# Two halves of the tokens in turns: another column order for TensorE's products, undone by VectorE

## The reference

```python
def first_block(x, mem, ...):
    # layer a: differential attention (6 heads of 2 x 64) + attention to 256 memory rows
    h = _rmsnorm(x, a_norm_attn)
    z = h @ a_w_in                                   # q, k, v, memory q
    x = x + concat([o_self, o_mem]) @ a_w_out
    x = x + relu(_rmsnorm(x, a_norm_mlp) @ a_w_up) ** 2 @ a_w_down      # 1024 -> 4096 -> 1024
    # layer b: the same with 12 causal heads; k and v from w_kv, q from b_w_in
    return _rmsnorm(x, final_norm)

def second_block(x, ...):
    # layer sb: stick-breaking attention, 16 heads of 64; layer fox: forgetting attention
    q, k, v = split(a @ w_qkv); h = h + rmsnorm(merge(o) @ w_o, post_g)
    # after each: a gated MLP with a causal convolution of 3 taps over the tokens
    f = conv_ffn(rmsnorm(h, ffn_pre_g), w_up, conv_w, conv_b, w_down)   # 1024 -> 2 x 2816 -> 1024
    h = h + rmsnorm(f, ffn_post_g)
```

## Time and profile before

| | us |
|---|---|
| median of three runs | 1201.98 |
| lowest and highest | 1201.56, 1206.76 |
| the profiled execution | 1206.9 |
| its span in the trace | 1205.1 |
| TensorE busy | 1188.5 |
| VectorE busy | 892.2 |
| ScalarE busy | 759.7 |
| GpSimd busy | 326.8 |

### The profile page before, as it was taken

How to read it: one execution, slowest core, us unless ns; L and a number is a source line. 1 busy time by engine, 2 the same in 40 slices (tenths; PEclk the granted TensorE clock), 3 DMA queues, 4 the chain that set the end, 5 groups by cost and what they waited for, 6 DMA issues and landing times.

```text
span 1205.1 us, 26850 instructions
## 1 busy us (share of the span) xinstructions
PE 1188.5 (99%) x9150; PEld 1105.7 (92%) x9150; DVE 892.2 (74%) x1491; ACT 759.7 (63%) x1373; POOL 326.8 (27%) x303
## 2 busy tenths in 40 slices
PE   9999999999999999999999999999999999999998
PEld 8888999999988999999998789999878988999986
DVE  7788877655578877666569979987456776999953
ACT  7666655444555655455557788887456665988842
POOL 3320355300012255432202105433000210455500
PEclk9999999999999999999999999999999999999999
DMA  8554465566545465655643345555645743566662
GB/s 319 176 155 145 162 206 192 177 206 202 198 144 156 151 196 194 217 185 190 209 157 118 136 152 192 191 186 192 198 139 170 241 134 125 189 195 204 194 209 89
DMA packets 64055, 216.64 MB, mean 180 GB/s; under 512 B 7776, under 2 KB 10992, under 8 KB 63984
## 3 DMA queue, kind: packets, MB, share of 16 engines
q1 hardware_dynamic: 63808, 215.17, 54.6%
q10 hardware_dynamic: 176, 0.54, 0.2%
HBM read 211.47 MB, written 1.06 MB: 176 GB/s over the span
## 4 chain that ended last, share of the span: by engine, by line
PE 87%; DVE 9%; ACT 2%; issue 1%; DMA 1%; POOL 0%; SPq 0%; DVEq 0%; ACTq 0%; POOLq 0%
PE bank L773 16%; PE bank L775 16%; PE bank L774 16%; PE bank L700 4%; PE bank L701 4%; PE bank L702 4%; PE bank L649 4%; PE bank L650 3%; PE bank L651 3%; DVE w_lo L1589 3%; PE bank L578 2%; PE bank L579 2%; PE bank L584 2%; PE bank L920 1%; PE bank L903 1%
## 5 line engine op out<-in xcount | busy, mean ns | idle before, releaser
L1127 ACT CAST w_hi<-raw 128x1024 fp32r<-128x1024 f32 x386 | 403.1, 1048 | 282.8 <-PE bank L775 129.5
L1589 DVE TENSOR_TENSOR w_lo<-raw,w_hi 128x1024 fp32r<-128x1024 f32 x386 | 504.4, 1316 | 88.6 <-ACT w_hi L1127 88.3
L773 PE MATMUL bank<-h_hi,w_hi 128*128 128x256 f32 x1184 | 329.7, 278 | 0.2
L775 PE MATMUL bank<-h_hi,w_lo 128*128 128x256 f32 x1184 | 328.5, 277 | 0.0
L774 PE MATMUL bank<-h_lo,w_hi 128*128 128x256 f32 x1184 | 328.5, 277 | 0.0
L773 PEld LDWEIGHTS bank<-h_hi,w_hi 128*128 128x128 f32 x1184 | 223.7, 189 | 1.1 <-DVE h_lo L1662 1.0
L774 PEld LDWEIGHTS bank<-h_lo,w_hi 128*128 128x128 f32 x1184 | 222.3, 188 | 0.1
L775 PEld LDWEIGHTS bank<-h_hi,w_lo 128*128 128x128 f32 x1184 | 222.3, 188 | 0.0
L773 PE MATMUL bank<-a_hi,w_hi 128*128 128x256 f32 x544 | 150.6, 277 | 1.1 <-DVE a_lo L1662 1.0
L775 PE MATMUL bank<-a_hi,w_lo 128*128 128x256 f32 x544 | 150.2, 276 | 0.0
L774 PE MATMUL bank<-a_lo,w_hi 128*128 128x256 f32 x544 | 150.2, 276 | 0.0
(11 more groups left out here) (222 smaller groups left out, 2108.5 us busy)
## 6 DMA issues: line engine op xcount, KB each, us to landing
raw<-in_w_up_sb SPq DMA_DIRECT2D x44, 512.0 KB, 3.5
raw<-in_w_up_fox SPq DMA_DIRECT2D x44, 512.0 KB, 4.2
raw<-in_w_up_a SPq DMA_DIRECT2D x32, 512.0 KB, 3.5
raw<-in_w_down_a SPq DMA_DIRECT2D x32, 512.0 KB, 4.6
raw<-in_w_up_b SPq DMA_DIRECT2D x32, 512.0 KB, 4.1
raw<-in_w_down_b SPq DMA_DIRECT2D x32, 512.0 KB, 4.6
raw<-in_w_in_sb SPq DMA_DIRECT2D x24, 512.0 KB, 3.7
raw<-in_w_in_fox SPq DMA_DIRECT2D x24, 512.0 KB, 3.6
```

Of the source, the lines that this page charges most:

```text
L773: nc.tensor.matmul(dst, w_hi[:, slot, w], src_hi[:, at + k, :], start=begin, stop=False)
L775: last = nc.tensor.matmul(dst, w_lo[:, slot, w], src_hi[:, at + k, :], start=False, stop=end)
L1127: nc.scalar.copy(w_hi[:, slot, 0:k * P], raw[:, slot, 0:k * P]).then_inc(hi_ready, 1)
L1589: nc.vector.tensor_tensor(w_lo[:, slot, 0:k * P], raw[:, slot, 0:k * P], w_hi[:, slot, 0:k * P].bitcast(f32), ALU.subtract).then_inc(lo_re ...
```

## The change

The moving operand of every feature-major product gets another order of columns. `in_turns` turns a tile's 256 tokens into the order 0, 128, 1, 129, ... 127, 255: the two halves of 128 tokens in turns. The matmul still writes its columns to PSUM one after the other, so a bank now holds the tokens in that order. Each eviction puts them back: it reads PSUM in two runs of 128 columns with a step of two (`product`), beside the two contiguous halves of its other operand and of its destination (`halves_of`). All buffers in SBUF keep their layout. Token-major products, attention, norms and transposes are not changed. No instruction is added, removed or put elsewhere.

```diff
+        def in_turns(x):
+            return x.rearrange("p (h a) -> p a h", h=2)
+        def halves_of(x):
+            return x.rearrange("p (h a) -> p h a", h=2)
+        def product(b):
+            return bank[b][:, 0:TOK].rearrange("p (a h) -> p h a", h=2)
...
-                            nc.tensor.matmul(dst, w_hi[:, slot, w], src_hi[:, at + k, :], start=begin, stop=False)
-                            nc.tensor.matmul(dst, w_hi[:, slot, w], src_lo[:, at + k, :], start=False, stop=False)
-                            last = nc.tensor.matmul(dst, w_lo[:, slot, w], src_hi[:, at + k, :], start=False,
+                            nc.tensor.matmul(dst, w_hi[:, slot, w], in_turns(src_hi[:, at + k, :]), start=begin, stop=False)
+                            nc.tensor.matmul(dst, w_hi[:, slot, w], in_turns(src_lo[:, at + k, :]), start=False, stop=False)
+                            last = nc.tensor.matmul(dst, w_lo[:, slot, w], in_turns(src_hi[:, at + k, :]), start=False,
                                                     stop=end)
...
-                nc.vector.tensor_tensor(dst, bank[s % 2][:, 0:TOK], scale[:], ALU.mult).then_inc(tile_out, 1)
+                nc.vector.tensor_tensor(halves_of(dst), product(s % 2), halves_of(scale[:]),
+                                        ALU.mult).then_inc(tile_out, 1)
...
-                    x = X[:, i * per + b, :]
-                    src = bank[OUT_BANK[b]] if name.startswith("out") else bank[b]
-                    nc.vector.tensor_tensor(x, src[:, 0:TOK], x, ALU.add).then_inc(tile_out, 1)
+                    x = halves_of(X[:, i * per + b, :])
+                    nc.vector.tensor_tensor(x, product(b), x, ALU.add).then_inc(tile_out, 1)
...
-                    nc.vector.scalar_tensor_tensor(u_buf[:, b, :], bank[b][:, 0:TOK], 0.0, rstd[:], ALU.max,
-                                                   ALU.mult).then_inc(tile_out, 1)
+                    nc.vector.scalar_tensor_tensor(halves_of(u_buf[:, b, :]), product(b), 0.0, halves_of(rstd[:]),
+                                                   ALU.max, ALU.mult).then_inc(tile_out, 1)
```

More of the change, by code:

```diff
@@ L648, in query_key_tile @@
                     dst, slot = bank[s % 2][:, 0:TOK], unit % RING
-                    nc.tensor.matmul(dst, w_hi[:, slot, w], src_hi[:, k, :], start=k == 0, stop=False)
-                    nc.tensor.matmul(dst, w_hi[:, slot, w], src_lo[:, k, :], start=False, stop=False)
-                    last = nc.tensor.matmul(dst, w_lo[:, slot, w], src_hi[:, k, :], start=False, stop=k == KT - 1)
+                    nc.tensor.matmul(dst, w_hi[:, slot, w], in_turns(src_hi[:, k, :]), start=k == 0, stop=False)
+                    nc.tensor.matmul(dst, w_hi[:, slot, w], in_turns(src_lo[:, k, :]), start=False, stop=False)
+                    last = nc.tensor.matmul(dst, w_lo[:, slot, w], in_turns(src_hi[:, k, :]), start=False, stop=k == KT - 1)
                 last.then_inc(units_done, 1)
@@ L720, in out_part @@
                     w = slice(k * P, (k + 1) * P)
-                    nc.tensor.matmul(dst, w_hi[:, slot, w], o_hi[:, k, :], start=k == MEMORY_K[0], stop=False)
-                    nc.tensor.matmul(dst, w_hi[:, slot, w], o_lo[:, k, :], start=False, stop=False)
-                    last = nc.tensor.matmul(dst, w_lo[:, slot, w], o_hi[:, k, :], start=False, stop=k == LAST_K)
+                    nc.tensor.matmul(dst, w_hi[:, slot, w], in_turns(o_hi[:, k, :]), start=k == MEMORY_K[0], stop=False)
+                    nc.tensor.matmul(dst, w_hi[:, slot, w], in_turns(o_lo[:, k, :]), start=False, stop=False)
+                    last = nc.tensor.matmul(dst, w_lo[:, slot, w], in_turns(o_hi[:, k, :]), start=False, stop=k == LAST_K)
                     if k == LAST_K:
@@ L737, in out_tiles @@
                         w = slice(k * P, (k + 1) * P)
-                        nc.tensor.matmul(dst, w_hi[:, slot, w], o_hi[:, k, :], start=k == 0, stop=False)
-                        nc.tensor.matmul(dst, w_hi[:, slot, w], o_lo[:, k, :], start=False, stop=False)
-                        last = nc.tensor.matmul(dst, w_lo[:, slot, w], o_hi[:, k, :], start=False, stop=k == KT - 1)
+                        nc.tensor.matmul(dst, w_hi[:, slot, w], in_turns(o_hi[:, k, :]), start=k == 0, stop=False)
+                        nc.tensor.matmul(dst, w_hi[:, slot, w], in_turns(o_lo[:, k, :]), start=False, stop=False)
+                        last = nc.tensor.matmul(dst, w_lo[:, slot, w], in_turns(o_hi[:, k, :]), start=False, stop=k == KT - 1)
                     last.then_inc(units_done, 1)
@@ L793, in together @@
                             dst, slot = bank[s][:, 0:TOK], (g["unit"] + s) % RING
-                            nc.tensor.matmul(dst, w_hi[:, slot, w], src_hi[:, k, :], start=k == 0, stop=False)
-                            nc.tensor.matmul(dst, w_lo[:, slot, w], src_hi[:, k, :], start=False, stop=False)
+                            nc.tensor.matmul(dst, w_hi[:, slot, w], in_turns(src_hi[:, k, :]), start=k == 0, stop=False)
+                            nc.tensor.matmul(dst, w_lo[:, slot, w], in_turns(src_hi[:, k, :]), start=False, stop=False)
                         pe.wait_ge(h_lo, operand_count(name, 0, 0, k))
@@ L798, in together @@
                             dst, slot = bank[s][:, 0:TOK], (g["unit"] + s) % RING
-                            last = nc.tensor.matmul(dst, w_hi[:, slot, w], src_lo[:, k, :], start=False,
+                            last = nc.tensor.matmul(dst, w_hi[:, slot, w], in_turns(src_lo[:, k, :]), start=False,
                                                     stop=k == KT - 1)
@@ L1035, in _ @@
                 dst = bank[6][:, 0:TOK]
-                nc.tensor.matmul(dst, wf_hi[:, k, :], h1_hi[:, k, :], start=k == 0, stop=False)
-                nc.tensor.matmul(dst, wf_hi[:, k, :], h1_lo[:, k, :], start=False, stop=False)
-                last = nc.tensor.matmul(dst, wf_lo[:, k, :], h1_hi[:, k, :], start=False, stop=k == KT - 1)
+                nc.tensor.matmul(dst, wf_hi[:, k, :], in_turns(h1_hi[:, k, :]), start=k == 0, stop=False)
+                nc.tensor.matmul(dst, wf_hi[:, k, :], in_turns(h1_lo[:, k, :]), start=False, stop=False)
+                last = nc.tensor.matmul(dst, wf_lo[:, k, :], in_turns(h1_hi[:, k, :]), start=False, stop=k == KT - 1)
             last.then_inc(f_logits, 1)
@@ L1655, in take_memory @@
                 dve.wait_ge(units_done, u + 1)
-                nc.vector.tensor_copy(Z[:, 8 + u, :], bank[u][:, 0:TOK]).then_inc(tile_out, 1)
+                nc.vector.tensor_copy(halves_of(Z[:, 8 + u, :]), product(u)).then_inc(tile_out, 1)
             def low(name, src, dst_hi, dst_lo, i, per, k):
@@ L1732, in before @@
                         dve.wait_ge(tap1_ready, i * 4 + (tap0 + b - 1))
-                    nc.vector.tensor_tensor(u_buf[:, b % 2, :], bank[b][:, 0:TOK], rstd[:],
+                    nc.vector.tensor_tensor(halves_of(u_buf[:, b % 2, :]), product(b), halves_of(rstd[:]),
                                             ALU.mult).then_inc(tile_out, 1)
@@ L2062, in _ @@
             dve.wait_ge(rstd_ready, NORMS["in_fox"] + 1)
-            link(nc.vector.tensor_tensor(f_x, bank[6][:, 0:TOK], rstd[:], ALU.mult))
+            link(nc.vector.tensor_tensor(halves_of(f_x), product(6), halves_of(rstd[:]), ALU.mult))
             link(nc.vector.tensor_scalar(f_x, f_x, b_f[:], -1.0, ALU.add, ALU.mult))
```

4 lines of the change are left out of this document (2 added, 2 removed).

## The result

The changed kernel takes 1188.55 us, median of 4 runs (1187.67 to 1189.56), against 1201.77 for the kernel before in the same session (4 runs, 1201.16 to 1206.76): ratio 0.9881, interval 0.9854 to 0.9909. The profiled spans are 1186.5 and 1205.1 us. It is faster, by 13 us where 35 were forecast. To read the two spans together one must know that the times of the kernel before fall in two groups, about 1201 to 1203 and 1205 to 1211 us, and that its profiled run (1206.9) is of the second.

A forecast was written before the change was run, and what follows sets the result against it. TensorE's pitch was taken as the bound, its float32r stream held up by SBUF reads: 40.2 us saved on 7224 products, evictions nothing, 4 us given back, so 36 off 1206.9 or the median, forecast 1167 us (chance 0.45), range 1149 to 1450.

The forecast's parts named there:

- cases of the other sign: Slower outcomes, 0.37 in all: evictions at half rate 1215 us (0.09), column fetch (0.29) from 1208 to 1946 us.
- my own range: Range of the likeliest case, 1149 us (pitch 106.7 ns) to 1190 (half the gain, or the gain with slow evictions).
- The stream is held up by the order of its reads: TensorE's float32r columns are held up some 4 to 10% by SBUF reads, and how the two reads stand matters.
- a constant distance to the weights' read: In turns the activation read advances at the weight load's rate, so the two SBUF reads never meet and the loss goes.
- The pitch of 109: All 7224 changed 256-column products would start 109 ns apart, as the float32 transposes do, saving 40.2 us together.
- the 4128 products at 113.3: First-block MLP products (4 x 768) and up_fox (1056) would save 4.3 ns each: 17.8 us.
- The 2040 among attention work: Products lying among attention work, taken at the middle pitch of 115.5 ns, would save 6.5 ns each: 13.3 us.
- up_sb's 8.6 ns: The stage up_sb has 1056 products at 117.6 ns, which at 109 would save 9.1 us.
- The evictions at nothing: 253 VectorE evictions reading PSUM with a step of two would cost nothing; rival at half rate +13 us, chance 0.09.
- 4 us given back: Taken off the gain for VectorE becoming the bound in up_fox and up_sb, and for waits that hide nothing today.
- The column fetch for itself: Rival: each column gets nothing from its neighbour, 7224 x 103 ns = 744 us more, 1946 us; chance 0.29, partial forms included.
- line rule: SBUF lines of 16 bytes want two successive hits; every column here changes line, so time of the column-fetch rival's order.

The follow-up runs named there:

- TensorE alone: Kernel computing nothing of the reference, 46 stretches of 48 matmuls differing in column order, place, width or type: 256 columns in turns 111.67 ns, in order 113.33 to 120.0.

## Why the prediction was right in kind and wrong in size

The forecast of 1167 us lay 21.5 us below the measured 1188.55. That this is inside the range of 1149 to 1450 says little, since the range was made wide for cases of the other sign; inside my own range (up to 1190) it was by 1.5 us.

**What bounds the kernel: right.** TensorE's pitch was the thing to count, and the change moved the span by what the pitch of the 7224 products moved: 18.0 of 18.6 us between the profiled runs.

**The stream is held up by the order of its reads: right.** 113.33 to 120 in order, 111.67 in turns in each stage, with evictions alone worth nothing. My reason for it was wrong: not a constant distance to the weights' read. The distance of the runs and the place change nothing in turns, the number of weight columns only the last 2.5 ns, and the loss in order is there with 32 weight columns. Why two runs of single columns are free while pairs, fours, four runs and bf16 are not, and why the order of neighbours has several paces, stays open; so does whether the place counts by itself or against the weights', since the weights never moved. With the weights read at a step of two the pitch in turns was 118.3, so their read is not without effect.

**The pitch of 109: this step failed.** The prediction took "the nearest row of an unhindered stream", the float32 transposes of the earlier trace rows, as the floor. What they show is right for the stream (109.15 with 120 weight columns), but the row is of true float32, and the weight load of 128 float32r columns, 111.67 ns, is a second floor just above it. I had it in view in the earlier trace rows, each weight load starting 0.01 us after the product ahead, so one per product, and priced it nowhere. I had also called the transposes' weight loads "of the same size". They have as many columns, but they are quicker, 140 ns for one where the products' take 188, so their 109 ns says nothing of the pace at which float32r weights can be loaded:

```profile
L633 PEld LDWEIGHTS bank<-ident_sb,X x16: 138/140/142, 608.7 to 616.0; 128*128 128x128 f32 x16
```

```profile
L774 PEld LDWEIGHTS bank<-h_lo,w_hi 128*128 128x128 f32 x1184 | 222.3, 188 | 0.1
```

On all 7224 products the floor's 111.67 in place of 109 is 19.3 us, nearly all that is missing. Term by term: the 4128 products at 113.3 saved 1.66 ns each in place of 4.3, 6.9 us and not 17.8. The 2040 among attention work stood at 114.9 on the mean, not at 115.5, and saved 3.2 ns each in place of 6.5, 6.6 us and not 13.3. With 6.5 us of up_sb that makes the 19.9 by pitch, where I had 40.2.

**up_sb's 8.6 ns: a term read from one run.** It gave 6.5 us of the 9.1 in the profiled run, since it did stand at 117.78 there. But of these, 4.7 us (1056 x 4.45) are of that run's pace. Against a run whose up_sb stands at 113.33, as with the evictions changed alone, the products give 14.1 us, and the medians, whose before is of the quicker group, differ by 13.2. I had noticed that 113.3 and 117.6 came "with no difference in arithmetic or clock", and that the profiled run was at the upper edge, and did not put the two together.

**The evictions at nothing: right**, 416 to 422 ns.

**4 us given back: too much, and not where I put it.** Against the kernel with the evictions alone it was 1.7 us: 7224 x 2.10 = 15.2 by pitch, 13.5 of span. Between the two profiled runs it was 1.3 (19.9 and 18.6), there with 1.3 us of help from the 512-column products, which were quicker without having been changed. VectorE did not become the bound of up_fox: at 898 products it works 96.60 of 100 us, and its idle time did not vanish. Whether it would have at 915 no run shows; by this row it would work 98.4.

**The signs.** Counts in up_fox were to be 915, 884 or 470: 898, between forecast and nothing, which is the floor's mark. The rows of the matmuls were to fall to 272 ns and stand at 275 to 276. The weight-load rows were to keep 188 and show 192; I had called growth a sign that the reads meet more, yet the pitch fell, so that sign was none: TensorE alone shows 188 to 192 ns in order and 192 in turns. The 512-column products kept their pitch (230.5 and 229.2). The pitch in the up stages of the first block, which was to be the sign of being wrong if it did not fall, fell from 113.33 to 111.67.

**The rivals.** The column fetch for itself did not come, though it is what a step of two would have done: at 230 ns it would have cost some 7224 x 116 = 838 us, an estimate. The Trainium skill's line rule, which spoke for it, does not hold for this order; the Trainium skill's alternation of one stream between two regions in "Vector Engine (DVE) Microarchitecture Reference", section 5.2, which was free for VectorE, is what TensorE does here with float32r.

## What to carry to other kernels

When one loss is removed from a pipelined engine, list every stream that runs once per instruction (here the moving columns and the weight load) and price each at its own row before choosing the floor; the gain ends at the second longest. Where TensorE is the chain with float32r operands, compare the pitch with columns at the granted clock before anything else, since in order the 256-column product was 1.5 to 10.5% above the best pace, by place and by what ran ahead (113.3 to 123.4 against 111.67), and reading two halves in turns took that away at every place tried, at no cost to the reader of PSUM. A pace that differs between two stretches of equal work may be a chance of the run: take it from two profiles before it becomes a term. And where steps of a steady stream double, look at the granted clock of that stretch first.

## What the runs showed of the hardware that I had not expected

- float32r, 256 columns in order: 113.33 to 120.0 ns by the place of the activations in steps of 64 B, up to 123.4 in finer steps, and two paces, 113.33 and 117.8, at one place. In turns 111.67 at every place; 512 columns 226.7 to 233.3 against 215.8.
- The load of 128 float32r weight columns repeats every 111.67 ns at best; of 120 columns or fewer it hides under 109.15. Read with a step of two, the weights bring the same product in turns to 118.3. The Trainium skill, "TensorE: Matmul & The Clock Gate", in "Back-to-back issue gap" gives 2.5 ns above the column time for an isolated matmul and some 131 ns for each of a stream at 512 columns; here the first is what a steady stream in turns has at each width tried from 272 to 512 (215.85 at 512), and nothing quicker was seen.
- Single columns from two runs are free, pairs cost 168 ns, fours 127, four runs 143, a step of two 230 and of eight 218; bf16 in turns 243 where bf16 in order is at 109.15.
- 192 B of padding were worth 33 to 37 us to the kernel before and nothing to the changed one (1186.9 without, 1188.6 with).
- VectorE reads PSUM with a step of two float32 at its usual pace.
